# Experts' loop over single blocks, with the down product in three products of rounded parts

## The chip, the cores and the metric

One core of one Trainium2 chip. The metric is the device time of one execution in microseconds (us), lower is better. The kernel is launched once and computes the whole trunk.

## The reference

A trunk of two layers on 512 tokens of width 1024, all in float32. Layer 0 mixes by a Conformer convolution, layer 1 by dilated attention over a shared K/V. After each comes the part that this change touches, a mixture of 16 experts of hidden width 512, two of them for each token:

```python
a = jnp.einsum("td,edf->tef", t, w_gate)
u = jnp.einsum("td,edf->tef", t, w_up)
hid = jax.nn.silu(a) * u * gates[:, :, None].astype(t.dtype)
y = jnp.einsum("tef,efd->td", hid, w_down)
```

The kernel doesn't compute every expert for every token: it routes, gathers the rows of each expert, and adds the weighted results.

## The kernel before

**Blocks and pairs.** The tokens of each expert are cut into blocks of 128 slots. There are at least 16 blocks (one for each expert), and more where an expert has over 128 tokens. In this run layer 0 has 17 blocks and layer 1 has 16. `moe_sp`, `moe_pool`, `moe_act`, `moe_dve` and `moe_pe` hold what each engine does in order; the engines wait for each other by semaphores. The loop goes over pairs of blocks (block number 2i + b, with b = 0 or 1 also naming the buffer). The last pair stands behind the loop and is written apart; where `two` is 0 it holds one block. Layer 0 has 8 pairs in the loop, layer 1 has 7.

**One block.** Its rows (`xg[b]`, gathered by an indirect DMA of GpSimd) are transposed on TensorE. ScalarE rounds them to the type fp32r (`xgh`, "lead"), VectorE takes the remainder (`xgl`, "trail"). The same is done with the expert's gate and up weights: ScalarE copies `wg[b]` into `wgh` and `wu[b]` into `wuh` (one buffer each), in halves of 128x2048, and VectorE writes the remainder in place of the raw weight (`wgl[b]`, `wul[b]`). A product in rounded parts is then three matmuls of fp32r where there would be one of f32: high times high, high times low, low times high. `gate` and `up` are 24 such matmuls each, into banks 0 and 1. ScalarE takes the silu, VectorE multiplies (`hidden`), TensorE transposes the result into bank 2, and VectorE copies it to `hidT`. The **down product** is plain f32: 8 matmuls of 128x512, which the trace shows as 16 records:

```python
for ft in range(FT):
    ins = M.matmul(PS[3 + h][:, :], hidT[:, ft, :], wd[b][:, ft, h * 512:(h + 1) * 512],
                   start=ft == 0, stop=ft == FT - 1)
```

ScalarE copies banks 3 and 4 to `yst[b]` (`store_y`), and GpSimd scatters it to DRAM by an indirect DMA.

**Order on TensorE** in a pair (`pair` of `moe_pe`, L1878): gate 0, up 0, gate 1, transposed hidden 0, rows of the next block 0, up 1, down 0, transposed hidden 1, rows of the next block 1, down 1.

**Queues.** SP issues the weight loads of 2 MB each (`expert_loads`, L578) in the order gate, up, down of block 0, then of block 1, each behind a wait until the buffer's last product is done. GpSimd issues gather, scatter, gather, scatter, each behind its waits, and each after small operations of its own (L694, L699, L705, L708). Each engine, and each queue, takes its work in the order written.

**Before the loop**: routing writes the block lists; two gathers, the transposes of both blocks' rows, then gate 0. GpSimd clears the last pair's rows in DRAM from `zeros` (`clear`) behind the gathers of the second pair. **Behind the loop**: the last pair, whose result is spread by matmuls (`sum_rows`) and added to the residual.

Of the kernel before, what the change touches and what calls it, by code (L numbers as in the profile page):

```python
# [120 lines left out]
class Later:  # L121
# [6 lines left out]
    def at(self, n):  # L128
        return self.base + n


def build_program(nc, a):
# [7 lines left out]
    with ExitStack() as ctx:  # L140
# [131 lines left out]
        zeros = cut(SC, 2 * D, D)  # L272
        SUM_BANKS = (5, 7, 0, 1)
# [46 lines left out]
        col = rs(2 * NT)  # L320
        hr = rs(2 * NT, E)
        big = rs16(2 * NT * MAXC * E).rearrange("p (a b c) -> p a b c", a=2 * NT, b=MAXC)
        over = rs(MAXC - 1, E)
# [4 lines left out]
        match = rs(XB, MAXC - 1, E)  # L328
# [136 lines left out]
        spread_mm, spread_sb = Later(var_mm, KT), Later(sig_done, KT)  # L465
        y_added, y_cleared = Later(taps_done, len(BY_TAPS)), Later(sem("y_cleared"), 0)
# [14 lines left out]
        def _(sp):  # L481
# [66 lines left out]
            def moe_sp(l):  # L548
# [29 lines left out]
                def expert_loads(i, bs, uses):  # L578

                    for b in bs:  # L580
                        j = sp.value_load(blk_e[0:1, bass.ds(2 * i + b, 1)], min_val=0, max_val=E - 1) + l * E
                        for dst, name, s, used in ((wg, "w_gate", wg_in, gate_mm), (wu, "w_up", wu_in, up_mm), (wd, "w_down", wd_in, down_mm)):
                            sp.wait_ge(used[l], uses + b)
                            expert_load(l, j, b, dst, name, s)

                with sp.Fori(1, last) as i:
                    expert_loads(i, (0, 1), 2 * i - 1)
                expert_loads(last, (0,), 2 * before + 1)
                with sp.If(two > 0):
                    expert_loads(last, (1,), 2 * before + 1)  # L590
# [59 lines left out]
        def _(pool):  # L650
# [21 lines left out]
            def moe_pool(l):  # L672
# [56 lines left out]

# [4 lines left out]
                def pair(i, more):  # L734

                    if not isinstance(i, int):
                        stored(i)
# [49 lines left out]
        def _(act):  # L787
# [140 lines left out]
            def moe_act(l):  # L928
# [6 lines left out]
                def lead(src, dst, w_in, done, n):  # L935

                    act.wait_ge(w_in, n * 16)
                    for q in range(2):
# [3 lines left out]
                def gate_lead(b, n, used):  # L942
                    if used is not None:
                        act.wait_ge(gate_mm[l], used)
                    lead(wg[b], wgh, wg_in[l][b], gh_done[l], n)
# [6 lines left out]
                def rows_lead(b, n):  # L952

                    act.wait_ge(xgT_mm[l][b], n)
                    for q in range(2):
                        nc.scalar.activation(xgh[b][:, 4 * q:4 * q + 4, :], PS[ROW_BANKS[b][q]][:, :].rearrange("p (a b) -> p a b", a=4),
# [4 lines left out]
                for b in range(2):  # L961
                    rows_lead(b, 1)
# [4 lines left out]
                def pair(i, more):  # L967
                    def silu_gate(b):
                        act.wait_ge(gate_mm[l], 2 * i + (b + 1))
                        act.wait_ge(hid_done[l], 2 * i + (b + 1))  # L970
                        nc.scalar.activation(sil, PS[0][:, :], ACT.Silu).then_inc(sil_done[l], 1)

                    def store_y(b):
                        to = yst[b] if more else yst[0]
                        act.wait_ge(down_mm[l], 2 * i + (b + 1))
                        act.wait_ge(y_free[l], i + 1)
                        nc.scalar.activation(to[:, 0:512], PS[3][:, :], ACT.Copy)
                        nc.scalar.activation(to[:, 512:1024], PS[4][:, :], ACT.Copy).then_inc(y_done[l], 1)  # L978

                    silu_gate(0)  # L980
                    if more:
                        gate_lead(1, i + 1, 2 * i + 1)
                        up_lead(1, i + 1, 2 * i + 1)
                        silu_gate(1)
                        gate_lead(0, i + 2, 2 * i + 2)
                        rows_lead(0, i + 2)
                        up_lead(0, i + 2, 2 * i + 2)
                        store_y(0)
                        rows_lead(1, i + 2)
                        store_y(1)  # L990
                    else:
                        def copy_hidT(b):
                            act.wait_ge(hT_mm[l], 2 * i + (b + 1))
                            if b == 1:
                                act.wait_ge(down_mm[l], 2 * i + 1)
                            nc.scalar.activation(hidT.rearrange("p a b -> p (a b)"), PS[2][:, :], ACT.Copy).then_inc(hidT_done[l], 1)  # L996

                        with act.If(two > 0):
                            gate_lead(1, i + 1, 2 * i + 1)
                            up_lead(1, i + 1, 2 * i + 1)  # L1000
                            silu_gate(1)
                        copy_hidT(0)
                        act.wait_ge(spread_mm.sem, spread_mm.at(l + 1))
                        nc.scalar.activation(spread_w[0], PS[5][:, :], ACT.Copy).then_inc(spread_sb.sem, 1)
                        store_y(0)
                        with act.If(two > 0):
                            copy_hidT(1)
                            act.wait_ge(y_done[l], 2 * i + 2)
                            nc.scalar.activation(yst[1], yst[0], ACT.Copy)
                            nc.scalar.activation(spread_w[1], PS[5][:, :], ACT.Copy).then_inc(hidT_done[l], 1)  # L1010
                            act.wait_ge(hidT_done[l], 2 * i + 3)
                            nc.scalar.activation(spread_w[0], PS[6][:, :], ACT.Copy)
                            store_y(1)

                with act.Fori(0, last) as i:
                    pair(i, True)
                pair(last, False)
# [75 lines left out]
        def _(dve):  # L1093
# [369 lines left out]
            def moe_dve(l):  # L1463
# [12 lines left out]
                def up_trail(b, m):  # L1476
                    trail(wu[b], wuh, wul[b], uh_done[l], ul_done[l], m)

                def rows_trail(b, m):

                    for q in range(2):
                        dve.wait_ge(xh_done[l], 2 * m + (q + 1))
                        ins = V.tensor_tensor(xgl[b][:, 4 * q:4 * q + 4, :], PS[ROW_BANKS[b][q]][:, :].rearrange("p (a b) -> p a b", a=4),
# [3 lines left out]
                gate_trail(0, 0, [0])  # L1487
                mixing_weights(l)
                rows_trail(0, 0)
                two = dve.value_load(two_i[0:1, 0:1], min_val=0, max_val=1)  # L1490
                last = dve.value_load(last_i[0:1, 0:1], min_val=E // 2 - 1, max_val=(E + XB) // 2 - 1)
                gate_trail(0, 0, [1])
                rows_trail(1, 1)
# [16 lines left out]
                def pair(i, more):  # L1510
                    def hidden(b):
                        dve.wait_ge(sil_done[l], 2 * i + (b + 1))
                        dve.wait_ge(up_mm[l], 2 * i + (b + 1))
                        V.tensor_tensor(hid, PS[1][:, :], sil, ALU.mult).then_inc(hid_done[l], 1)

                    def copy_hidT(b):
                        dve.wait_ge(hT_mm[l], 2 * i + (b + 1))
                        if b == 1:
                            dve.wait_ge(down_mm[l], 2 * i + 1)
                        V.tensor_copy(hidT.rearrange("p a b -> p (a b)"), PS[2][:, :]).then_inc(hidT_done[l], 1)  # L1520

                    if more:
                        gate_trail(1, 2 * i + 1)
                        hidden(0)
                        up_trail(1, 2 * i + 1)
                        copy_hidT(0)
                        gate_trail(0, 2 * i + 2)
                        rows_trail(0, 2 * i + 2)
                        hidden(1)
                        copy_hidT(1)  # L1530
                        up_trail(0, 2 * i + 2)
                        rows_trail(1, 2 * i + 3)
                        dve.wait_ge(down_mm[l], 2 * i + 2)
                    else:
                        steps.wait()
                        for b in range(2):
                            place_last(b)
                        with dve.If(two > 0):
                            gate_trail(1, 2 * i + 1)
                        hidden(0)  # L1540
                        with dve.If(two > 0):
# [679 lines left out]
```

## Time and profile before

| | us |
|---|---|
| median of 3 runs (lowest, highest) | 1597.34 (1595.4, 1599.31) |
| the profiled execution, device time | 1596.6 |
| its span, first to last instruction | 1594.8 |
| TensorE busy in the span | 1530.2 (96%) |
| VectorE busy | 1077.8 (68%) |
| ScalarE busy | 677.4 (42%) |

The experts' loops take from 250 to 563 us (layer 0) and from 1257 to 1532 us (layer 1) of the span. Busy times overlap: an engine that is busy 96% of the span isn't idle for long anywhere, and a group's mean duration can be longer than the distance from one matmul to the next, since matmuls are pipelined.

### The profile page before, as it was taken

The page shows a single profiled execution, that of the slowest core. Times are in us where ns is not written, and L with a number is a line of the kernel's source. Part 1 is how long each engine was busy: PE and PEld are TensorE (multiplying, and loading weights), DVE is VectorE, ACT ScalarE, POOL GpSimd, SP SyncE. Part 2 cuts the span into 40 slices and gives each one's busy share as a digit, 9 for nine tenths or more (in the row PEclk, how much of TensorE's full clock was granted, in tenths as well). Part 3 has the DMA queues.
Part 4 walks back from the last instruction along what each step waited for, and adds up shares of the span by engine and source line. Part 5 has one row for each costly group of instructions (what it writes and reads, how often), then busy time and mean ns, then how long its engine had stood idle before and what let it go on. Part 6 is the DMA issues. An engine that isn't in the chain of part 4 may idle for free.

```text
span 1594.8 us, 19902 instructions
## 1 busy us (share of the span) xinstructions
PE 1530.2 (96%) x7320; PEld 1181.0 (74%) x7320; DVE 1077.8 (68%) x1327; ACT 677.4 (42%) x742; POOL 411.9 (26%) x351
## 2 busy tenths in 40 slices
PE   6989888999999989999999999999999799999997
PEld 5878676666666657888888888888888566666663
DVE  6997748555555579586767767586772955555566
ACT  4111636455555534423323241423333555555552
POOL 4000025222222217150513224150501522222220
PEclk9999989999999999999999999999999899999999
DMA  5233425888888863121212121221435578888873
GB/s 216 73 126 98 193 106 233 330 335 340 345 354 351 342 273 105 64 79 39 92 41 90 53 79 53 66 79 40 170 129 219 197 295 352 346 359 339 356 283 132
DMA packets 52535, 309.85 MB, mean 194 GB/s; under 512 B 10512, under 2 KB 16272, under 8 KB 38672
## 3 DMA queue, kind: packets, MB, share of 16 engines
q1 hardware_dynamic: 41840, 291.28, 46.6%
q0 software_dynamic: 9792, 16.80, 2.9%
q10 hardware_dynamic: 864, 1.26, 0.2%
q8 instruction: 24, 0.39, 0.1%
q14 instruction: 15, 0.12, 0.0%
HBM read 299.33 MB, written 28.84 MB: 206 GB/s over the span
## 4 chain that ended last, share of the span: by engine, by line
PE 78%; DVE 9%; DMA 8%; ACT 2%; issue 2%; SPq 0%; POOL 0%; DVEq 0%; ACTq 0%; POOLq 0%
PE PS L1913 12%; PE PS L2000 5%; PE PS L2002 5%; PE PS L2001 5%; PE PS L2085 3%; PE PS L1888 3%; DMA WR<-w_gate 3%; DMA WR<-w_up 3%; PE PS L2101 3%; PE PS L1892 3%; PE PS L1889 3%; PE PS L1875 3%; PE PS L1873 3%; PE PS L2016 3%; PE PS L2018 3%; PE PS L2017 3%
## 5 line engine op out<-in xcount | busy, mean ns | idle before, releaser
L1471 DVE TENSOR_TENSOR wgl<-WR,wgh 128x2048 fp32r<-128x2048 f32 x66 | 148.5, 2289 | 208.0 <-ACT wgh L940 206.9
L778 POOL TENSOR_TENSOR KQ<-rope_ab 64x512 f32<-64x512 f32 x96 | 173.6, 1809 | 364.8 <-DVE rope_ab L1583 361.2
L1913 PE MATMUL PS<-WR,SC 128*128 128x512 f32 x528 | 233.2, 594 | 2.6 <-ACT SC L996 1.3
L1025 ACT ACTIVATE wh<-wraw 128x1024 fp32r<-128x1024 f32 x76 | 80.3, 1058 | 249.5 <-PE PS L2002 248.7
L1913 PEld LDWEIGHTS PS<-WR,SC 128*128 128x128 f32 x528 | 98.8, 190 | 116.6 <-issue 114.5
L1471 DVE TENSOR_TENSOR wul<-WR,wuh 128x2048 fp32r<-128x2048 f32 x66 | 148.1, 2285 | 0.1
L940 ACT ACTIVATE wgh<-WR 128x2048 fp32r<-128x2048 f32 x66 | 122.4, 1904 | 60.4 <-DMA WR<-w_gate 60.4
L940 ACT ACTIVATE wuh<-WR 128x2048 fp32r<-128x2048 f32 x66 | 122.7, 1906 | 29.2 <-PE PS L1875 20.3
L1583 DVE TENSOR_TENSOR rope_ab<-PS,rope_sb 32x512 f32<-32x512 f32 x192 | 131.9, 687 | 2.6
L1888 PE MATMUL PS<-wgh,xgh 128*128 128x512 f32 x264 | 111.4, 422 | 1.0 <-DVE wgl L1471 1.0
L1565 DVE TENSOR_TENSOR wl<-wraw,wh 128x1024 fp32r<-128x1024 f32 x76 | 93.1, 1225 | 28.0 <-ACT wh L1025 26.3
L1873 PE MATMUL PS<-wuh,xgh 128*128 128x512 f32 x264 | 104.4, 395 | 0.0
L1889 PE MATMUL PS<-wgl,xgh 128*128 128x512 f32 x264 | 103.6, 392 | 0.0
L1875 PE MATMUL PS<-wuh,xgl 128*128 128x512 f32 x264 | 103.0, 390 | 0.0
L1874 PE MATMUL PS<-wul,xgh 128*128 128x512 f32 x264 | 102.7, 389 | 0.0
L1625 DVE RECIPROCAL rope_ab<-PS 64x512 f32<-64x512 f32 x16 | 53.7, 3359 | 61.8 <-PE PS L2101 61.6
L2000 PE MATMUL PS<-HQh,wh 128*128 128x512 f32 x192 | 76.3, 398 | 4.6 <-DVE HTl L1127 2.6
L708 POOL TENSOR_TENSOR idle<-ident_sb 128x1 f32<-128x1 f32 x30 | 34.2, 1140 | 165.4 <-ACT SC L978 165.4
L2016 PE MATMUL PS<-HTh,wh 128*128 128x512 f32 x192 | 76.2, 397 | 0.0
L2002 PE MATMUL PS<-HQh,wl 128*128 128x512 f32 x192 | 75.6, 394 | 0.0
L2001 PE MATMUL PS<-HQl,wh 128*128 128x512 f32 x192 | 75.4, 393 | 0.0
L2018 PE MATMUL PS<-HTh,wl 128*128 128x512 f32 x192 | 74.8, 390 | 0.0
(323 smaller groups left out, 3307.8 us busy)
## 6 DMA issues: line engine op xcount, KB each, us to landing
WR<-w_gate SPq DMA_DIRECT2D x33, 2048.0 KB, 12.1
WR<-w_up SPq DMA_DIRECT2D x33, 2048.0 KB, 16.7
WR<-w_down SPq DMA_DIRECT2D x33, 2048.0 KB, 8.3
wraw<-w_qkv SPq DMA_DIRECT2D x72, 512.0 KB, 3.3
WR<-w_in SPq DMA_DIRECT2D x8, 1024.0 KB, 4.9
xn_dram<-SC SPq DMA_DIRECT2D x8, 512.0 KB, 2.8
SC<-y_dram SPq DMA_DIRECT2D x8, 512.0 KB, 5.8
HT<-y_dram SPq DMA_DIRECT2D x8, 512.0 KB, 9.4
```

Source lines behind the costliest of these rows:

```text
L778: nc.gpsimd.tensor_tensor(to, cos, sin, ALU.add).then_inc(rope_done, 1)
L940: nc.scalar.activation(dst[:, kts, :], src[:, kts, :], ACT.Copy).then_inc(done, 1)
L1471: V.tensor_tensor(lo[:, kts, :], raw[:, kts, :], hi[:, kts, :].bitcast(F32), ALU.subtract).then_inc(done, 1)
L1583: ins = V.tensor_tensor(rope_ab[d:d + 32, 2 * (t % 2) + 1, :], src[s:s + 32, :], rope_t[s:s + 32, tab + 1, :], ALU.mult)
L1873: M.matmul(dst, xgh[b][:, kt, :], hi[:, kt, :], start=kt == 0, stop=False)
L1875: ins = M.matmul(dst, xgl[b][:, kt, :], hi[:, kt, :], start=False, stop=kt == KT - 1)
L1888: M.matmul(PS[0][:, :], xgh[b][:, kt, :], wgh[:, kt, :], start=kt == 0, stop=False)
L1889: M.matmul(PS[0][:, :], xgh[b][:, kt, :], wgl[b][:, kt, :], start=False, stop=False)
L1913: ins = M.matmul(PS[3 + h][:, :], hidT[:, ft, :], wd[b][:, ft, h * 512:(h + 1) * 512], start=ft == 0, stop=ft == FT - 1)
L2000: M.matmul(PS[t % 2][:, :], whk, hi[:, kt, :], start=kt == 0, stop=False)
L2001: M.matmul(PS[t % 2][:, :], whk, lo[:, kt, :], start=False, stop=False)
L2002: ins = M.matmul(PS[t % 2][:, :], wlk, hi[:, kt, :], start=False, stop=kt == KT - 1)
```

## The change

The loop's body becomes one block: number 2i + c, with c = 1 and 2 written out, so that each pass of the hardware loop still covers two blocks. In it, the down product of the block before is done in two halves of 512 columns, one ahead of this block's up product and one behind it. Each half is 12 matmuls of fp32r (high-high, low-high, high-low), in place of 4 of f32. The hidden rows are split (`hTh` by ScalarE, `hTl` by VectorE), and so is the down weight: its high half goes to `wdh`, one buffer for both halves of columns, and the remainder to `wdl[b]`, in place of `wd[b]`. With n blocks, blocks 0 to n-3 (17 blocks) or 0 to n-4 (16 blocks) get the split down product: 15 in layer 0 and 13 in layer 1. The last block of the loop and the last pair keep the f32 form.

Buffers, and one moved table (`match` made room for `hTl`); `wdh` lies over `zeros`, `hTh` over `hidT`:

```diff
+        wdh = at("wdh", 184, [P, FT, 512], F32R)
+        wdl = [at(f"wdl{b}", 112 + 16 * b, [P, FT, D], F32R) for b in range(2)]
+        hTh = at("hTh", 196, [P, FT, P], F32R)
...
+        hTl = at("hTl", 32 + o / 256, [P, FT, P], F32R)
```

SP: the down load of a block is issued one block later in the queue.

```diff
-                with sp.Fori(1, last) as i:
-                    expert_loads(i, (0, 1), 2 * i - 1)
-                expert_loads(last, (0,), 2 * before + 1)
...
+                gate_up_loads(1, 0, 1)
+                gate_up_loads(1, 1, 1)
+                down_load(1, 0, 1)
+                with sp.Fori(2, last) as i:
+                    gate_up_loads(i, 0, 2 * i - 1)
+                    down_load(i - 1, 1, 2 * i - 3)
+                    gate_up_loads(i, 1, 2 * i - 1)
+                    down_load(i, 0, 2 * i - 1)
```

GpSimd: the clears go ahead of the second pair's gathers; the wait for the stored rows stands in each scatter, and in ScalarE's copies, in place of `stored(i)` at the head of a pair.

```diff
                 def scatter(b, n):
+                    if not isinstance(n, int):
+                        pool.wait_ge(y_stored[l][b], n * 16)
...
                 for b in range(2):
+                    clear(b)
+                for b in range(2):
                     pool.wait_ge(gathered[l][b], 16)
                     gather(b, 1)
-                for b in range(2):
-                    clear(b)
```

ScalarE, one block:

```diff
+                def split_block(i, c):
+                    p, n = (c - 1) % 2, (c + 1) % 2
+                    act.wait_ge(hT_mm[l], 2 * i + c)
+                    nc.scalar.activation(hTh[:, :, :].rearrange("p a b -> p (a b)"), PS[2][:, :], ACT.Copy).then_inc(hTh_done[l].sem, 1)
+                    act.wait_ge(wd_in[l][p], (i + 1) * 16)
+                    if isinstance(i, int) and i == 0 and c == 1:
+                        act.wait_ge(y_cleared.sem, y_cleared.at(32 * (l + 1)))
+                    down_lead(0, i, p)
+                    silu_gate(i, c)
+                    gate_lead(n, i + 2, None, [0])
+                    act.wait_ge(down_half[l].sem, down_half[l].at(2 * i + c))
+                    down_lead(1, i, p)
+                    gate_lead(n, i + 2, None, [1])
+                    if not isinstance(i, int):
+                        act.wait_ge(y_stored[l][p], i * 16)
+                    nc.scalar.activation(yst[p][:, 0:512], PS[3][:, :], ACT.Copy)
+                    rows_lead(n, i + 2)
+                    up_lead(n, i + 2, 2 * i + (c + 1))
+                    act.wait_ge(down_mm[l], 2 * i + c)
+                    nc.scalar.activation(yst[p][:, 512:1024], PS[4][:, :], ACT.Copy).then_inc(y_done[l], 1)
```

VectorE, one block (ahead of the loop, `gate_trail(0, 0)` and `rows_trail(0, 0)` now stand in front of `mixing_weights`):

```diff
+                def split_block(i, c, between=None):
+                    n, m = (c + 1) % 2, 2 * i + (c + 1)
+                    dve.wait_ge(hTh_done[l].sem, hTh_done[l].at(2 * i + c))
+                    V.tensor_tensor(hTl[:, :, :].rearrange("p a b -> p (a b)"), PS[2][:, :],
+                                    hTh[:, :, :].rearrange("p a b -> p (a b)").bitcast(F32), ALU.subtract).then_inc(hidT_done[l], 1)
+                    down_trail(0, i, c)
+                    gate_trail(n, m, [0])
+                    down_trail(1, i, c)
+                    gate_trail(n, m, [1])
+                    hidden(i, c)
+                    rows_trail(n, m)
+                    up_trail(n, m, [0])
+                    if between is not None:
+                        between()
+                    up_trail(n, m, [1])
```

TensorE: half a down product, one block, and the order around the loop (`transpose_rows(1, 1)` was ahead of gate 0).

```diff
+                def split_down(h, i, c):
+                    b, to = (c - 1) % 2, PS[3 + h][:, :]
+                    pe.wait_ge(dh_done[l].sem, dh_done[l].at(4 * i + (2 * c - 1 + h)))
+                    if h == 0:
+                        pe.wait_ge(hidT_done[l], 2 * i + c)
+                        pe.wait_ge(y_done[l], 2 * i + c)
+                    for ft in range(FT):
+                        M.matmul(to, hTh[:, ft, :], wdh[:, ft, :], start=ft == 0, stop=False)
+                        M.matmul(to, hTl[:, ft, :], wdh[:, ft, :], start=False, stop=False)
+                    pe.wait_ge(dl_done[l].sem, dl_done[l].at(4 * i + (2 * c - 1 + h)))
+                    for ft in range(FT):
+                        ins = M.matmul(to, hTh[:, ft, :], wdl[b][:, ft, h * 512:(h + 1) * 512], start=False, stop=ft == FT - 1)
...
+                def split_block(i, c):
+                    gate(i, c)
+                    transpose_rows((c + 1) % 2, i + 2)
+                    split_down(0, i, c)
+                    up(i, c)
+                    split_down(1, i, c)
+                    transpose_hidden(i, c)
+
+                gate(0, 0)
+                transpose_rows(1, 1)
+                up(0, 0)
+                transpose_hidden(0, 0)
+                with pe.Fori(0, before) as i:
+                    for c in (1, 2):
+                        split_block(i, c)
+                split_block(before, 1)
+                transpose_rows(1, before + 2, 1)
+                down(before, 1)
```

The rows of all blocks in the loop now go through the same two banks (`banks=0`); the last pair's block 1 keeps its own.

## Rows read from the trace of the kernel before

**Rows 1.** The page: busy times of the engines, and DMA share and rate by slice.
```profile
PE 1530.2 (96%) x7320; PEld 1181.0 (74%) x7320; DVE 1077.8 (68%) x1327; ACT 677.4 (42%) x742; POOL 411.9 (26%) x351
DMA  5233425888888863121212121221435578888873
GB/s 216 73 126 98 193 106 233 330 335 340 345 354 351 342 273 105 64 79 39 92 41 90 53 79 53 66 79 40 170 129 219 197 295 352 346 359 339 356 283 132
```

**Rows 2.** Windows, one for each pair: width, busy us by engine, clock, DMA share, GB/s.
```profile
399.80:438.60 38.80, 38.69 (x152) 26.78 (x153) 22.66 (x17) 21.34 (x20) 9.48 (x13) 1.00 0.84 348
438.60:478.00 39.40, 38.99 (x152) 26.75 (x152) 22.65 (x17) 21.32 (x20) 9.50 (x13) 1.00 0.87 356
1407.90:1446.60 38.70, 38.70 (x153) 26.91 (x154) 22.55 (x17) 21.34 (x19) 9.59 (x14) 1.00 0.82 343
```

**Rows 3.** The chain of waits in a pair: start us, us, what.
```profile
421.58 1.83 PE PS L1892 x8
...
430.26 6.87 PE PS L1913 x16
437.13 0.47 PE PS L1904 x4
437.60 0.90 PE PS L1862 x8
...
451.36 16.59 DMA WR<-w_gate
```

**Rows 4.** Timeline, TensorE, last down product of each loop: start us, us, operation.
```profile
555.53 7.11 PE L1913 MATMUL PS<-WR,SC 128*128 128x512 f32 x16
1524.96 7.10 PE L1913 MATMUL PS<-WR,SC 128*128 128x512 f32 x16
```

**Rows 5.** Timeline, ScalarE, in one pair.
```profile
438.53 1.08 ACT L956 ACTIVATE xgh<-PS 128x512 fp32r<-128x512 f32 x2
446.24 0.59 ACT L978 ACTIVATE SC<-PS 128x512 f32<-128x512 f32 x1
446.85 1.28 ACT L971 ACT_TABLE_LOAD   x1
451.73 3.71 ACT L940 ACTIVATE wgh<-WR 128x2048 fp32r<-128x2048 f32 x2
```

**Rows 6.** Timeline, VectorE, in one pair.
```profile
453.67 4.49 DVE L1471 TENSOR_TENSOR wgl<-WR,wgh 128x2048 fp32r<-128x2048 f32 x2 [9.74 <-ACT wgh L940]
458.08 0.68 DVE L1514 TENSOR_TENSOR SC<-PS,SC 128x512 f32<-128x512 f32 x1
474.34 1.28 DVE L1483 TENSOR_TENSOR xgl<-PS,xgh 128x512 fp32r<-128x512 f32 x2
```

**Rows 7.** Windows of 2 us inside a pair (columns as in group 2).
```profile
401.75:403.70 1.95, 1.95 (x6) 0.80 (x5) 1.95 (x1) 0.00 (x0) 1.80 (x2) 1.00 1.06 454
...
427.10:429.05 1.95, 1.95 (x10) 1.60 (x10) 0.00 (x0) 0.50 (x1) 1.34 (x3) 1.00 0.98 420
...
434.90:436.85 1.95, 1.95 (x6) 0.69 (x5) 1.89 (x4) 1.95 (x2) 0.00 (x0) 1.00 0.00 0
```

**Rows 8.** Weight loads between 321 and 560 us, issue to landing.
```profile
DMA to landing us min/median/max: 7.5/15.9/17.7
```

**Rows 9.** Timeline, GpSimd: small operations and issues, beside and without VectorE's work.
```profile
253.72 2.19 POOL L721 COPY HTQ<-HTQ 128x1 uint32 x1
...
401.91 2.89 POOL L709 DMA_INDIRECT y_dram<-SC,HTQ  x1 [0.15 <-issue]
404.81 0.19 POOL L694 COPY HTQ<-HTQ 128x1 uint32 x1
...
408.82 1.01 POOL L709 DMA_INDIRECT y_dram<-SC,HTQ  x1 [0.51 <-issue]
```

**Rows 10.** Timeline at both loops' starts: TensorE, then GpSimd.
```profile
248.57 1.97 PE L1862 MATMUL PS<-ident_sb,SC 128*128 128x128 f32 x8 [1.17 <-DMA SC<-xn_dram,HTQ]
250.20 0.78 PE L1888 MATMUL PS<-wgh,xgh 128*128 128x512 f32 x1
1256.74 0.48 PE L1888 MATMUL PS<-wgh,xgh 128*128 128x512 f32 x1
243.65 1.04 POOL L700 DMA_INDIRECT SC<-xn_dram,HTQ  x1 [0.17 <-issue]
```

**Rows 11.** DMA issues between 252.6 and 252.8 us: the gather of a second-pair block.
```profile
SC<-xn_dram,HTQ POOLq DMA_INDIRECT x1, 12.9
```

More of the change, by code:

```diff
@@ L960, in moe_act @@
                 up_lead(0, 1, None)
-                for b in range(2):
-                    rows_lead(b, 1)
+                rows_lead(0, 1)
                 act.wait_ge(routed.sem, routed.at(l, 1))
@@ L965, in moe_act @@
                 last = act.value_load(last_i[0:1, 0:1], min_val=E // 2 - 1, max_val=(E + XB) // 2 - 1)
[L967 to L971, printed above, removed]
+                before = act.value_load(last_i[0:1, 1:2], min_val=E // 2 - 2, max_val=(E + XB) // 2 - 2)
@@ new lines, in moe_act @@
+                silu_gate(0, 0)
+                gate_lead(1, 1, 1)
+                rows_lead(1, 1)
+                up_lead(1, 1, 1)
+                for c in (1, 2):
+                    split_block(0, c)
+                with act.Fori(1, before) as i:
+                    for c in (1, 2):
+                        split_block(i, c)
+                split_block(before, 1)
+                rows_lead(1, before + 2, 1)
+                act.wait_ge(down_mm[l], 2 * before + 2)
+                act.wait_ge(y_stored[l][1], before * 16)
@@ L982, in pair @@
+                    with act.If(two > 0):
                         gate_lead(1, i + 1, 2 * i + 1)
                         up_lead(1, i + 1, 2 * i + 1)
[L984 to L989, printed above, removed]
-                        store_y(1)
[L991 to L1013, printed above, removed]
@@ L1019, in _ @@
+                last_pair(last)
             moe_act(0)
@@ L1508, in place_last, with hidden @@
                         V.tensor_tensor(to, to, part, ALU.add).then_inc(spread_set.sem, 1)
[L1510 to L1522, printed above, removed]
+                def hidden(i, c):
+                    dve.wait_ge(sil_done[l], 2 * i + (c + 1))
+                    dve.wait_ge(up_mm[l], 2 * i + (c + 1))
+                    V.tensor_tensor(hid, PS[1][:, :], sil, ALU.mult).then_inc(hid_done[l], 1)
@@ new lines, in copy_hidT @@
+                def copy_hidT():
+                    dve.wait_ge(hT_mm[l], 2 * before + 2)
+                    V.tensor_copy(hidT.rearrange("p a b -> p (a b)"), PS[2][:, :]).then_inc(hidT_done[l], 1)
+                gate_trail(1, 1)
+                hidden(0, 0)
+                rows_trail(1, 1)
+                up_trail(1, 1)
+                with dve.Fori(0, before) as i:
+                    for c in (1, 2):
+                        split_block(i, c)
+                split_block(before, 1, copy_hidT)
@@ L1523, in pair, with last_pair @@
+                rows_trail(1, 2 * before + 3, 1)
+                def last_pair(i):
+                    steps.wait()
+                    for b in range(2):
+                        place_last(b)
+                    with dve.If(two > 0):
                         gate_trail(1, 2 * i + 1)
-                        hidden(0)
+                    hidden(i, 0)
+                    with dve.If(two > 0):
                         up_trail(1, 2 * i + 1)
-                        copy_hidT(0)
-                        gate_trail(0, 2 * i + 2)
@@ L1528, in pair @@
[L1528 to L1541, printed above, removed]
-                            up_trail(1, 2 * i + 1)
-                            hidden(1)
-                        for n in range(NT):
-                            add_stored(n, l)
-                        dve.wait_ge(y_added.sem, y_added.at((l + 1) * NT))
-                        with dve.If(two > 0):
-                            for n in range(NT):
-                                for h in range(2):
-                                    dve.wait_ge(sum_mm[l].sem, sum_mm[l].at(2 * n + h + 1))
-                                    add_sum(n, h).then_inc(sum_add[l].sem, 1)
@@ L1553, in moe_dve @@
-                with dve.Fori(0, last) as i:
-                    pair(i, True)
-                pair(last, False)
+                        hidden(i, 1)
+                    for n in range(NT):
+                        add_stored(n, l)
+                    dve.wait_ge(y_added.sem, y_added.at((l + 1) * NT))
+                    with dve.If(two > 0):
+                        for n in range(NT):
+                            for h in range(2):
+                                dve.wait_ge(sum_mm[l].sem, sum_mm[l].at(2 * n + h + 1))
+                                add_sum(n, h).then_inc(sum_add[l].sem, 1)
@@ L1556, in moe_dve @@
+                last_pair(last)
                 return two
@@ L1963, in moe_pe, with gate @@
-                with pe.Fori(0, last) as i:
-                    pair(i, True)
-                pair(last, False)
+                def gate(i, c):
+                    b = c % 2
+                    if c > 0:
+                        pe.wait_ge(sil_done[l], 2 * i + c)
+                    for kt in range(KT):
+                        if kt % half == 0:
+                            pe.wait_ge(xh_done[l], 4 * i + (2 * c + kt // half + 1))
+                            pe.wait_ge(gl_done[l], 4 * i + (2 * c + kt // half + 1))
+                        M.matmul(PS[0][:, :], xgh[b][:, kt, :], wgh[:, kt, :], start=kt == 0, stop=False)
+                        M.matmul(PS[0][:, :], xgh[b][:, kt, :], wgl[b][:, kt, :], start=False, stop=False)
+                    pe.wait_ge(xl_done[l], 2 * i + (c + 1))
+                    for kt in range(KT):
+                        ins = M.matmul(PS[0][:, :], xgl[b][:, kt, :], wgh[:, kt, :], start=False, stop=kt == KT - 1)
+                    ins.then_inc(gate_mm[l], 1)
@@ new lines, in down @@
+                def down(i, b):
+                    pe.wait_ge(wd_in[l][b], (i + 1) * 16)
+                    pe.wait_ge(hidT_done[l], 2 * i + (b + 1))
+                    pe.wait_ge(y_done[l], 2 * i + (b + 1))
+                    for h in range(2):
+                        for ft in range(FT):
+                            ins = M.matmul(PS[3 + h][:, :], hidT[:, ft, :], wd[b][:, ft, h * 512:(h + 1) * 512],
+                                           start=ft == 0, stop=ft == FT - 1)
+                    ins.then_inc(down_mm[l], 1)
@@ L1967, in _ @@
+                last_pair(last)
             moe_pe(0)
```

235 lines of the change are left out of this document (124 added, 111 removed).

## The prediction

> **What bounds the kernel now.** I read the page first: TensorE is busy 96% of the span, and in the experts' slices the DMA engines stand at eight tenths with 330 to 359 GB/s [rows 1]. Then windows, one for each pair of blocks: TensorE is busy for 38.7 to 39.0 us of 38.7 to 39.4, at a granted clock of 1.00; VectorE for 22.7, ScalarE for 21.3 [rows 2]. The chain of waits says what a pair is made of: 8 matmuls of fp32r in 1.83 us (0.228 us each), the transposed hidden rows 0.47, the next rows 0.90, and the f32 down product 6.87, or 7.1 where it stands behind a wait [rows 3, 4]. A DMA appears in it only now and then: a gate weight, 16.59 us from issue to landing, holds ScalarE's rounding [rows 3], and with it some pairs last 39.4 instead of 38.7. So the loop is bound by TensorE, and a block costs 2 x 5.48 (gate, up) + 6.98 (down) + 0.47 + 0.90 = 19.3 us. I also looked at what must grow: ScalarE's and VectorE's operations [rows 5, 6], the DMA rate inside a pair [rows 7, 8], and GpSimd's small operations [rows 9].
>
> **The down product.** Removed: 6.98 us. Added: 24 matmuls x 0.228 = 5.46, same shape as gate's. The trace has no fp32r product with `wdh`, so bounds: if each half pays the start behind a wait, some 0.1 each, 5.7; if an fp32r matmul here went no faster than half an f32 one (6.87 / 16 = 0.43), 10.3; below, 24 x 0.22 = 5.3, since no row has it faster. I take 5.46 and put the waits in a term of their own. The gain is 1.52 a block, on the path, for 15 + 13 = 28 blocks: **42.6 us**.
>
> **TensorE's waits.** A block will have 16 waits instead of 13, and the down product in two pieces. Old pairs lose 38.7 - 38.6 = 0.1 to this. I take 0.15 a block (bounds 0 and 0.5), so a block lasts 5.48 + 0.90 + 2.73 + 5.48 + 2.73 + 0.47 + 0.15 = **17.95 us**, against 19.35 to 19.7 now.
>
> **Does the rest fit into 17.95?** Walk one block, with 0 at the end of the transposed hidden rows of the block before. TensorE: gate to 5.5, rows to 6.4, first half of down to 9.2, up to 14.7, second half to 17.4, hidden transposed to 17.95.
> ScalarE: leads are 3.71 for two halves, a PSUM copy 0.59 (pitch 0.5), rows 1.08 [rows 5]. The up weight's lead and the last copy of the block before run to about 1.2; `hTh` to 1.7; down lead to 3.6; silu at 5.5 to 6.1; gate lead, first half, to 7.9; behind the wait for the first half of down (9.2), down lead to 11.0; gate lead to 12.9; copy, rows to 14.5; behind up (14.7), the up lead to 18.4; last copy to 18.9, which is 0.95 of the next block: it closes. Sum 14.6, and one table load of 1.28 [rows 5] a pass, hidden in the gap between 3.6 and 5.5. Were it two, silu ends at 6.7, still harmless.
> VectorE: trails are 4.49 for two halves, 0.68 for an operation on PSUM, rows 1.28 [rows 6]. The up trails end at 4.0; `hTl` 4.6; down trail 6.9; gate trail (lead at 7.9) 10.2; down trail (11.0) 13.3; gate trail 15.6; hidden 16.2; rows 17.5; up trails (leads at 16.6, 18.4) to 21.9, which is 4.0 again. Sum 3 x 4.49 + 1.28 + 2 x 0.68 = 16.1 of 17.95. TensorE needs the down trail at 8.2 (spare 1.3), the up trails at 9.2 (5), hidden at 17.4 (1.2), the gate trail at 17.95 (2.3). The thinnest cover is 1.2 us; each us beyond it costs 28 us in all. The old table copy to `hidT` is gone, `hTl` takes its place.
> So ScalarE's added 3.7 + 0.5 and VectorE's added 4.5 lie beside TensorE's work, and I cost them at nothing.
>
> **Loads.** All three of a block's weights still move; SP's queue is past nothing that has to come earlier: gate at 5.5, up at 14.7, down at 17.4, in order of time. A pair moves 348 GB/s x 38.8 us = 13.5 MB [rows 2]. In the 14 windows of 2 us from 401.8 to 429.0 the engines stand at a share of 1 and move 405 to 460 GB/s, mean about 428; near 435 they are empty [rows 7], because four of a pair's six loads wait for the second half of it. At 428 a pair needs 31.5 us, a block 15.8; with what lies between landings I reckon 17.0, under 17.95. Each load may take about 18 us from its issue until ScalarE wants it (gate: 5.5 to 6.1 of the next block, 18.5; up 17.9; down 20). The longest now is 17.7 [rows 8], behind a backlog of three loads that the new order, spread over the block, doesn't build. So the wait for the gate weight goes too: old pairs of layer 0 last 312.4 / 8 = 39.05 on average [rows 4, 10], 0.35 over 38.7; this is in the end points below.
>
> The Trainium skill, "SBUF — State Buffer", summary of rules for kernel authors, says to reckon with about 358 GB/s between HBM and SBUF. By it a pair would need 37.7 us and a block 18.9, and DMA would take TensorE's place; the trace's 428 over 27 us disagrees, though no slice of 40 us has more than the rule gives, hence rival 1.
>
> **Ends of the loops.** Layer 0 now: gate 0 starts at 250.2 behind the second block's rows [rows 10], the last pair at 555.53 + 7.0 = 562.5 [rows 4]. New: gate 0 needn't wait for the second rows, 248.7; rows, up 0, then one idle us for `hidden`; first block of the loop at 262.2; 15 x 17.95 = 269.3; then rows 0.9, a wait of 0.9 for `hidT` (VectorE's first up trail is ahead of it) and 7.0 of f32. That gives 540.3, plus the start's gather. The second pair's gather is issued behind two clears: from 243.65 + 1.04 [rows 10] six small steps of 2.2 and issues of 1.0 to 2.9 [rows 9] bring it to about 261.5, where it was at 252.7. Its landing took 12.9 then behind the down loads [rows 11], it may take 5 to 13 now; TensorE wants the rows at 268.6. Stall 0 to 6, I take 2.5: 542.8, so **19.7** saved. Layer 1: 1256.74 to 1532.0 now [rows 4, 10]; new first block at 1269.5, 13 x 17.95 = 233.4, stall 1, 8.8: 1512.7, **19.3** saved. What follows the loops is as before: the last loads are issued at the same distance from the last pair.
>
> **Sum.** 1596.6 - 39 = 1557.6, in the profiled execution's own time; it lies 0.7 under the median of the runs, so **1558**. With waits at 0 and no stalls it would be 1549; with waits at 0.5 a block and stalls of 6, 1573.
>
> **Rivals.**
> 1. DMA paces the block. For: the share is already 0.84 to 0.87 [rows 2], and no slice has over 359 GB/s [rows 1]. Against: the windows at 428 [rows 7]. If 359 were the limit, 13.5 MB take 37.6 us, 18.8 a block: 28 x 0.85 = 24 over the forecast, 1582.
> 2. GpSimd starves, the slower side. Its small operations take 0.19 us alone and 2.2 under a trail, an issue 1.0 and 2.9 [rows 9]. VectorE's trails grow from 9 to 13.5 us a block, so each step may meet one: four steps and two issues, 4 x 2.2 + 5.8 + gaps = 16, just inside a block. If each step waited for two trails (4.5), 4 x 4.5 + 5.8 = 23.8 a block: the rows and `yst` come late, and 28 x (23.8 - 19.4) = 123 are lost: 1720. It decides from 19.4 us a block on, 3.4 a step. Against: at 253.72 VectorE was busy all the while and the step took 2.19.
> 3. The products don't pay: 24 fp32r matmuls take what 16 f32 records take (0.29 each). Then only the stalls go, about 5 us: 1592. Against: gate's 0.228, with operands laid out the same way.
>
> The Trainium skill, "SBUF — State Buffer", section "Who interferes with whom", has it that a VectorE instruction with two SBUF inputs and a GpSimd instruction that reads SBUF exclude each other for the whole instruction. The trace agrees as to one trail (2.19 against 0.19); it speaks against this change as far as rival 2 goes, whose two trails in a row no row shows.
>
> **How the numbers follow.** Forecast 0.72, rival 1 (or another 0.3 to 1 us a block) 0.16, rival 2 0.05, rival 3 0.04, and 0.03 for a failed cover that costs more than all gains. The forecast's own range is 1549 to 1570; with part of rival 1 it is 1549 to 1577. A difference under 0.2% (3 us) can't be told from none. Faster 0.90, same 0.03, slower 0.07.
>
> **What would show it.** Pairs of 35.9 us in windows from the third block on, TensorE idle in them for under 0.3; down's fp32r matmuls at 0.228 pitch; DMA share about 0.92 at 375 GB/s; VectorE at 32 us a pair. A stall of TensorE at the transposed hidden rows says that VectorE has no cover; ScalarE waiting for weights says rival 1; TensorE waiting for gathered rows in mid-loop, or ScalarE for stored rows, says rival 2. I am wrong if a pair takes over 37.

## The result, and the profile after

The changed kernel takes **1560.3 us** (median of 4 runs, 1559.8 to 1560.7), against 1597.6 for the kernel before: a ratio of 0.976, 95% interval 0.975 to 0.9775. The forecast was 1558, with a range of 1549 to 1577. The profiled execution's span is 1558.6 us, 36.2 less than before.

The page of the changed kernel, the lines that answer to [rows 1]:

```profile
PE 1489.0 (96%) x7544; PEld 1223.9 (79%) x7544; DVE 1200.9 (77%) x1383; ACT 773.2 (50%) x813; POOL 488.3 (31%) x338
...
DMA  5242517899999663121212121212256389999973
GB/s 194 95 134 83 213 52 287 347 373 370 377 393 391 253 262 95 55 81 40 94 40 81 54 81 54 81 54 67 72 199 246 115 335 367 387 380 383 365 279 124
```

TensorE is still busy 96% of a shorter span; VectorE and ScalarE have taken up the roundings, and the DMA digits in the experts' slices went from 8 to 9. Windows, one for each two blocks, answer to [rows 2]:

```profile
391.94:427.59 35.65, 35.65 (x170) 29.77 (x169) 31.58 (x21) 28.13 (x25) 16.80 (x12) 1.00 0.95 380
427.59:463.25 35.66, 35.66 (x170) 29.77 (x169) 31.59 (x21) 28.16 (x25) 16.80 (x12) 1.00 0.97 393
...
1379.42:1415.07 35.65, 35.65 (x170) 29.77 (x169) 31.59 (x21) 28.14 (x25) 16.80 (x12) 1.00 0.95 377
```

Two blocks take 35.65 us, 17.83 a block, and TensorE isn't idle in them at all. Every split block but the first of each loop lasts 17.82 or 17.83. The long pairs that waited for a gate weight are gone. The chain of waits in one block holds TensorE alone (start us, us, what; the answer to [rows 3]):

```profile
395.61 1.82 PE PS L1954 x8
397.43 0.88 PE PS L1927 x8
...
400.17 0.91 PE PS L1990 x4
408.39 0.91 PE PS L1990 x4
409.30 0.47 PE PS L1966 x4
```

VectorE's timeline in the same block shows how it fits between: the hidden product (L1561) ends at 408.17, and TensorE begins the transposes at 409.30 in the chain. VectorE's only gaps are those in brackets, 1.17 and 0.88 us:

```profile
395.85 0.68 DVE L1572 TENSOR_TENSOR hTl<-PS,hTh 128x512 fp32r<-128x512 f32 x1
396.45 2.28 DVE L1567 TENSOR_TENSOR wdl<-WR,wdh 128x2048 fp32r<-128x2048 f32 x1
399.90 2.29 DVE L1520 TENSOR_TENSOR wgl<-WR,wgh 128x2048 fp32r<-128x2048 f32 x1 [1.17 <-ACT wgh L963]
403.07 2.29 DVE L1567 TENSOR_TENSOR wdl<-WR,wdh 128x2048 fp32r<-128x2048 f32 x1 [0.88 <-ACT wdh L996]
405.28 2.28 DVE L1520 TENSOR_TENSOR wgl<-WR,wgh 128x2048 fp32r<-128x2048 f32 x1
407.48 0.69 DVE L1561 TENSOR_TENSOR SC<-PS,SC 128x512 f32<-128x512 f32 x1
```

Weight loads between 391 and 500 us, from issue to landing. Where it was 15.9 and at most 17.7 [rows 8], it is 11.0 and 12.1, with the issues spread over the block:

```profile
DMA to landing us min/median/max: 8.0/11.0/12.1
```

And the ends of the loops, TensorE's timeline: the first gate product of layer 0, the first transposed hidden rows, and the f32 product behind the split blocks (it answers to [rows 4] and [rows 10]):

```profile
251.20 0.79 PE L1950 MATMUL PS<-wgh,xgh 128*128 128x512 f32 x1 [0.69 <-ACT xgh L979]
...
266.42 0.75 PE L1966 MATMUL PS<-ident_sb,SC 128*128 128x128 f32 x4 [1.27 <-DVE SC L1561]
...
537.04 7.11 PE L1975 MATMUL PS<-WR,SC 128*128 128x512 f32 x16 [1.59 <-DVE SC L1587]
```

### The profile page after: what moved, and what is told of

Same layout as the page of the kernel before. It is cut to its first block, busy times and chain, and to the rows that moved or that the text cites. A ratio compares the mean times of both kernels' runs of the same rounds, so it can differ in the third digit from the quotient of the medians.

```text
span 1558.6 us, 20726 instructions
## 1 busy us (share of the span) xinstructions
PE 1489.0 (96%) x7544; PEld 1223.9 (79%) x7544; DVE 1200.9 (77%) x1383; ACT 773.2 (50%) x813; POOL 488.3 (31%) x338
## 4 chain that ended last, share of the span: by engine, by line
PE 85%; DVE 10%; issue 1%; DMA 1%; ACT 1%; DVEq 0%; SPq 0%; ACTq 0%; POOLq 0%
PE PS L2087 5%; PE PS L2089 5%; PE PS L2088 5%; PE PS L1950 4%; PE PS L1951 4%; PE PS L1954 4%; PE PS L2172 4%; PE PS L1939 3%; PE PS L1937 3%; PE PS L1938 3%; PE PS L1986 3%; PE PS L1987 3%; PE PS L2188 3%; PE PS L1990 3%; PE PS L2103 3%; PE PS L2105 3%
## 5 line engine op out<-in xcount | busy, mean ns | idle before, releaser
L1567 DVE TENSOR_TENSOR wdl<-WR,wdh 128x2048 fp32r<-128x2048 f32 x56 | 128.0, 2286 | 24.3 <-ACT wdh L996 24.3
L996 ACT ACTIVATE wdh<-WR 128x2048 fp32r<-128x2048 f32 x56 | 107.4, 1919 | 35.0 <-PE PS L1990 35.0
L1950 PE MATMUL PS<-wgh,xgh 128*128 128x512 f32 x264 | 107.8, 408 | 1.4 <-ACT xgh L979 1.4
L734 POOL TENSOR_TENSOR idle<-ident_sb 128x1 f32<-128x1 f32 x30 | 20.8, 694 | 260.9 <-ACT SC L1017 248.7
L1986 PE MATMUL PS<-wdh,hTh 128*128 128x512 f32 x224 | 91.1, 407 | 0.0
L1987 PE MATMUL PS<-wdh,hTl 128*128 128x512 f32 x224 | 88.2, 394 | 0.0
L735 POOL DMA_INDIRECT y_dram<-SC,HTQ x30 | 79.4, 2647 | 5.3 <-issue 5.3
```

The costliest lines, as they stand in the source:

```text
L1950: M.matmul(PS[0][:, :], xgh[b][:, kt, :], wgh[:, kt, :], start=kt == 0, stop=False)
L1986: M.matmul(to, hTh[:, ft, :], wdh[:, ft, :], start=ft == 0, stop=False)
L1987: M.matmul(to, hTl[:, ft, :], wdh[:, ft, :], start=False, stop=False)
```

## The experiments

Each was timed beside the kernel before on one chip. The changed kernel was run again beside the later ones (e5 to e10), since they differ from it by a few us; for e1 to e4 it stands at 1560.3 from the first chip.

**e1, the order alone.** The down product goes back to f32, in the new place:

```diff
-                        M.matmul(to, hTh[:, ft, :], wdh[:, ft, :], start=ft == 0, stop=False)
-                        M.matmul(to, hTl[:, ft, :], wdh[:, ft, :], start=False, stop=False)
...
+                        ins = M.matmul(to, hidT[:, ft, :], wd[b][:, ft, h * 512:(h + 1) * 512], start=ft == 0, stop=ft == FT - 1)
```

> The new order and the new queues, but the down product in f32 as before (two halves of 4 f32 matmuls, no hTh, hTl, wdh, wdl). Theory (the gain is the cheaper product, the order only hides its roundings): a block goes from 17.83 to 17.83 + 6.92 - 5.46 = 19.3 us, 28 blocks give back 41 us: about 1601, a little over the kernel before, whose pairs average 19.5 a block but whose loops start 2 to 3 us faster. Rival (the order itself saves, by ending the waits for weights and for the copy of the hidden rows): 1585 or less.

1592.7 us, ratio to before 0.9973 (0.9963 to 0.9982). The chain of e1 in one block:

```profile
400.27 0.47 PE PS L1956 x4
...
407.09 3.44 PE PS L1976 x8
...
416.00 3.43 PE PS L1976 x8
419.43 0.47 PE PS L1956 x4
```

From 400.27 to 419.43, from one set of transposed hidden rows to the next, a block lasts 19.16. So the cheaper product is worth 19.16 - 17.83 = 1.33 us a block (6.87 of f32 against 5.54), 37 us in 28 blocks, and the order, which ends the waits for weights and lets the f32 product run without a start behind a wait, 19.52 - 19.16 = 0.36, 10 us. In layer 0 e1 also lost 4.6 us once, in its first block: it came to the third block's rows at about 267.6 and they weren't there.

```profile
270.12 1.69 PE L1917 MATMUL PS<-ident_sb,SC 128*128 128x128 f32 x8 [2.51 <-DMA SC<-xn_dram,HTQ]
```

Most of the gain is the product's, as the theory had it. By the medians e1 is 4.1 us under the kernel before and the changed kernel is 37.3 under it, so the product brings some 33 and the order alone 4, where the theory had e1 at 4 over. The blocks' 10 us of the order don't all arrive: 4.6 of them go in that first block. The split product in the old order of pairs was not tried.

**e2, two of the three products.** It leaves out the low-high product of the split blocks:

```diff
-                        M.matmul(to, hTl[:, ft, :], wdh[:, ft, :], start=False, stop=False)
```

> Leaves out the low-high product of the down projection (8 of its 24 matmuls a block), all else as in the changed kernel, hTl included: shows what bounds a block next. TensorE then needs 17.83 - 1.82 = 16.0 us. Theory A (VectorE, 15.8 busy, with its order comes next): 16.1 to 16.5 a block, 28 x 1.3 to 1.7 less, 1513 to 1524. Theory B (DMA paces from the 17.0 that I reckoned from landings): 17.0 a block, 1537. Theory C (DMA can do no more than the 380 to 393 GB/s of now): 17.5 to 17.8 a block, 1551 to 1560.

1531.5 us, 16.73 a block, where TensorE's own work is 16.0. A window of two blocks, and the landing of weight loads issued between 280 and 310 us, and between 430 and 460:

```profile
382.50:416.00 33.50, 33.03 (x154) 26.53 (x152) 31.60 (x21) 28.17 (x25) 20.91 (x12) 1.00 0.99 403
```
```profile
DMA to landing us min/median/max: 7.8/10.8/11.5
...
DMA to landing us min/median/max: 13.1/17.0/17.9
```

The chain in it runs through VectorE and ScalarE (start us, us, what):

```profile
421.61 0.68 DVE hTl L1572
422.29 2.21 DVE wdl L1567
...
424.55 1.21 PE PS L1989 x4
425.76 0.02 issue
425.79 1.93 ACT wdh L996
```

The number lies between A (16.1 to 16.5) and B (17.0), and in neither; by the total B is even a little nearer. It is the chain that speaks for A's mechanism: no DMA is in it, and VectorE, busy 15.8 of 16.73, sets the pace together with the order in which it and ScalarE take the halves. What A had too small is the waiting between the two. C fell: the DMA engines moved 403 GB/s. B is half right. DMA doesn't end the chain, but its share is 0.99, and the median landing grew from 10.8 us to 17.0 in some 9 blocks, 0.7 a block; after that it stayed at 17.0 (460 to 490 us). By this growth DMA's own pace is some 17.4 us a block (an estimate from these two medians), and a longer loop would have used up the 18 us that a load may take. So behind TensorE's 17.83 stand DMA at about 17.4, which this loop is too short to feel, and VectorE at about 16.7. In the changed kernel the same medians stay between 9.2 and 12.0 over the whole loop.

**e3 and e5, VectorE's cover.** One more VectorE instruction ahead of the hidden product, over 280 columns (1.90 us) or 110 (0.84 us):

```diff
+                    V.reciprocal(PS[7][:, 0:280], hTh[:, :, :].rearrange("p a b -> p (a b)")[:, 0:280].bitcast(F32))
                     hidden(i, c)
```

> Adds one VectorE instruction (a reciprocal over 128x280, about 1.9 us by the 3.36 us of 64x512) ahead of the hidden product in each of the 28 split blocks. Theory (VectorE's cover ahead of the transposed hidden rows is 1.1 us, nothing else): each block grows by 1.9 - 1.1 = 0.8, 22 us in all: 1582. Rival (the walk's spare isn't the real one; since VectorE is then busy 17.7 of 17.83, queued waits add up): 1.9 a block or more, 1613. Rival (VectorE runs ahead and absorbs it): 1561.

> As e3, but a reciprocal over 128x110, about 0.75 to 0.8 us (from e3's 1.90 us for 280 columns). From e3 the cover is 1.83 - 1.09 = 0.75, where the walk had 1.1: theory (the cover is 0.75 to 0.85): blocks of 17.83 to 17.9, total 1560 to 1562. Rival (no cover: VectorE's time counts in full once it is near its limit): 0.75 a block, 1581.

e3: 1592.95 us, blocks of 18.82 and 19.0, 18.92 on average (the first of layer 0 20.78, with a wait of 1.67 for gathered rows in it). e5: 1563.1 us beside 1558.4 for the changed kernel on that chip, blocks of 17.82 to 17.99. TensorE waits at the transposed hidden rows (e3; waits in us, times, longest):

```profile
PE PS L1967 <- DVE SC L1561: 8.0, 11, 0.7
```

An instruction in a row takes some 0.08 less than its own time, so e3 added 1.82 and the block grew by 1.09; e5 added 0.76 and it grew by 0.06. Both give a cover of **0.7 us**, where the walk had 1.2 and TensorE's first transpose comes 1.1 behind VectorE's end. The weight loads (PEld) show why: the hidden rows are what the transposes load as weights, and in the changed kernel this load begins at 408.91, 0.74 behind VectorE's 408.17. In e3 it waits for VectorE (start us, us, and the idle time before it; first the changed kernel, then e3):

```profile
408.91 0.67 PEld L1966 LDWEIGHTS PS<-ident_sb,SC 128*128 128x128 f32 x4
...
396.83 0.56 PEld L1967 LDWEIGHTS PS<-ident_sb,SC 128*128 128x128 f32 x4 [1.15 <-DVE SC L1561]
```

Beyond the cover VectorE's time is paid in every block. The first theory of each run has the mechanism, with the cover too large: for e3 it said 0.8 a block and 1582, and 1.09 and 1593 came. In e5 the blocks make 1.6 of the 4.7 us over the changed kernel. In the profiled execution most of the rest is at the end of layer 0's loop: the copy for the f32 product came 0.7 later, and the product took 8.80 us instead of 7.11, at a granted clock of 0.50 from 537.5 to 540.5. In layer 1 it took 7.10.

**e4, the loads in the old order.** SP's queue again takes gate, up, down of a pair's block 0, then of block 1:

```diff
...
+                with sp.Fori(1, last) as i:
+                    for b in range(2):
+                        gate_up_loads(i, b, 2 * i - 1)
+                        down_load(i, b, 2 * i - 1)
...
```

> The changed kernel with SP's queue in the old order: gate, up, down of block 2i, then of block 2i+1. The down load of block 2i can only be issued at the end of block 2i+1's pass, and the gate load of block 2i+3's buffer stands behind it: 12 us later than now. Theory (the queue order is what keeps the loads off the path): gate weight lands 7 us too late once in a pair, half of it made good: 3.5 to 7 us a pair, 14 pairs: 50 to 95 us, 1610 to 1655. Rival (18 us of slack for a load that lands in 11 is enough): 1560 to 1565.

1646.3 us, ratio to before 1.031 (1.028 to 1.033): slower than before the change, with every other part of it in. Two of the waits between 300 and 500 us:

```profile
DVE wgl L1515 <- ACT wgh L958: 57.4, 10, 9.2
ACT wgh L958 <- DMA WR<-w_gate: 38.6, 9, 5.8
```

ScalarE waits for the gate weight, VectorE for ScalarE, and the blocks last about 21 us. The theory's 50 to 95 us came as 86 over the changed kernel. The split alone isn't the change; the queue that issues the down load a block later belongs to it.

**e7 and e8, the ends of the loops.** e7 moves VectorE's copy ahead of the up trails, its three register loads (2.3 us) behind the first up trail, and the first hidden product between the halves of a gate trail. e8 adds filler matmuls at the start. The last of e7's three edits, and e8's:

```diff
...
-                gate_trail(1, 1)
+                gate_trail(1, 1, [0])
                 hidden(0, 0)
+                gate_trail(1, 1, [1])
...
+                fill(8)
                 transpose_rows(0, 1)
+                fill(4)
```

> The changed kernel, with VectorE's copy of the hidden rows for the loop's last f32 down product ahead of both halves of the up trail, VectorE's three register loads behind the first up trail, and the first hidden product between the halves of the second block's gate trail. Theory (the ends of the loops are a chain through VectorE): the wait of 1.59 us ahead of the f32 product goes in both layers (3.2), the loops start 0.7 and 1.7 us earlier, unless the gathered rows of the third block are late then: 1554 to 1557. Rival (other waits end at the same time): within 1 us of the changed kernel.

> e7, and 8 matmuls of bf16 into a free bank ahead of the first rows' transposes and 4 behind them. In the changed kernel TensorE's granted clock was 0.50 from 251.2 to 255.2 us, behind an idle stretch, and 9 matmuls took 0.43 instead of 0.23 us there. Theory (with no idle stretch the clock stays up): 1.8 us less than e7 in layer 0, 1552 to 1555. Rival (the fillers themselves are on the path, or the first gather and not TensorE sets the start): same as e7 or 1 us more.

> The changed kernel once more beside these three, to compare on one chip: 1560 to 1561.

e7 took 1559.1 us, e8 1559.5, the changed kernel beside them 1558.4: nothing gained. TensorE's timeline of e7 shows why. It came to the transposes earlier and then waited at the down product of the first block, which lasted 19.92 instead of 17.93:

```profile
265.49 0.75 PE L1967 MATMUL PS<-ident_sb,SC 128*128 128x128 f32 x4 [0.85 <-DVE SC L1561]
...
273.93 0.47 PE L1987 MATMUL PS<-wdh,hTh 128*128 128x512 f32 x1 [1.31 <-issue]
```

At the start VectorE is the bound, and what I took from one place I put ahead of another (`hTl` at 273.15 in e7, 271.88 in the changed kernel). e8's filler made no difference to the time that can be measured, and its trace shows what it did:

```profile
246.14 2.74 PE L1933 MATMUL PS<-c_sb 128*128 128x384 bf16 x8 [2.03 <-issue]
248.67 1.30 PE L1928 MATMUL PS<-ident_sb,SC 128*128 128x128 f32 x8
...
250.65 0.50 PE L1957 MATMUL PS<-wgh,xgh 128*128 128x512 f32 x1
```

The gate product then ran at a granted clock of 1.00, where e7's first ones ran at 0.50. But the filler came behind TensorE's idle 2.03 us and not in it, ran at 0.50 itself, and stood ahead of the transposes for 2.5 us. From the start of a routing product that both have (`HTQ,c_sb`) to the first transposed hidden rows it is 30.8 us in e8 (232.84 to 263.60) and 31.0 in e7 (234.47 to 265.49). So it is the rival's first half: the filler is on the path, and costs what it gives back. The moved copy was still to be seen by itself, which led to e6.

**e6, the copy alone.**

```diff
+                    if between is not None:
+                        between()
                     up_trail(n, m, [0])
-                    if between is not None:
-                        between()
                     up_trail(n, m, [1])
```

> The changed kernel, with nothing moved but VectorE's copy of the hidden rows for the loop's last f32 down product, now ahead of both halves of the up trail. In e7 that wait went from 1.59 to 0.23 us, but the first block of each loop became 2.1 us longer. Theory (e7's start ate the gain of its end): 2 x 1.36 = 2.7 us less than the changed kernel, 1555.5 to 1556. Rival (the gain is given back behind the loop, where the last pair waits for the later up trail or the stored rows): within 1 us of it.

1555.3 us (1554.4 to 1556.5), beside 1559.3 (1557.4 to 1560.3) for the changed kernel: the fastest version here that has all three products. The f32 product behind the split blocks now waits 0.23 us instead of 1.59:

```profile
532.77 7.11 PE L1975 MATMUL PS<-WR,SC 128*128 128x512 f32 x16 [0.23 <-ACT SC L1017]
```

That accounts for 2.7 of the 4.0 us; the rest is no more than the difference between runs of one kernel: in the profiled executions e6's loop also starts 2.0 us earlier (248.53 against 250.50). The ratios to before (0.9741, 0.9727 to 0.9754, and 0.9761, 0.9748 to 0.9775) only just overlap.

**e10, GpSimd's cover.** Three small operations instead of one ahead of each gather and scatter:

```diff
-                        nc.gpsimd.tensor_tensor(idle[:, :], ident[:, 0:1], ident[:, 0:1], ALU.mult)
+                        for k in range(3):
+                            nc.gpsimd.tensor_tensor((idle, spare[:, 6:7], spare[:, 5:6])[k][:, :], ident[:, 0:1], ident[:, 0:1], ALU.mult)
```

> The changed kernel with three small GpSimd operations instead of one ahead of every gather and scatter of a block: 4 more a block, 0.2 to 2.2 us each. GpSimd waits 8.6 of 17.83 us a block for the stored rows, a gather lands some 12 and a scatter some 7 us ahead of need. Theory (it has that much cover): no change, 1558 to 1561. Rival 2 of the prediction (its steps each meet a trail, and the rows come late): over 5 us slower.

> The changed kernel beside these two, on the same chip: 1558 to 1561.

1557.9 us beside 1559.3: no change. GpSimd's timeline, one issue in the changed kernel, then e10:

```profile
393.94 2.90 POOL L735 DMA_INDIRECT y_dram<-SC,HTQ  x1 [0.16 <-issue]
...
392.78 0.69 POOL L736 TENSOR_TENSOR idle<-ident_sb 128x1 f32<-128x1 f32 x1 [8.65 <-ACT SC L1019]
393.43 2.39 POOL L736 TENSOR_TENSOR spare<-ident_sb 128x1 f32<-128x1 f32 x2
395.97 1.02 POOL L737 DMA_INDIRECT y_dram<-SC,HTQ  x1 [0.15 <-issue]
```

Its two extra steps took 2.39 us together, and the issue behind them 1.02 instead of the 2.90 it takes in the changed kernel. Both wait out the same trail of VectorE: it ends at 395.6 in e10, the steps at 395.8; it ends at 395.9 in the changed kernel, the issue at 396.8. So more steps don't mean more waiting. It still idles for 8.65 us a block.

## Why the prediction was right, point by point

**What bounds the kernel**: right. TensorE, before and after; the experts' loops gave 18.5 + 18.1 us of the span's 36.2, the stages between them took 0.5 more and those behind them 0.1 less.

**The down product**: 1.52 a block was forecast, e1 has 1.33. I took the mean of 6.87 and 7.1; the 7.1 holds a start behind a wait, which belongs to the order. The rest is on the new side, where I had 5.46 and 5.54 came. The term is 37 us and not 42.6.

**TensorE's waits and the old pairs' stalls**: 17.95 a block was forecast, 17.83 measured. The parts of the chain, 5.49 + 0.88 + 2.77 + 5.44 + 2.78 + 0.47, add up to all of it, so the 0.15 for waits was nothing. The gain against the old average of 19.52 is 1.69 a block and 47 us in all, 10 of them from the order. That is 3.4 over the forecast's 44, and the ends of the loops kept 6 more than forecast (below). That the total came within 2.3 us of 1558 is in part luck: two errors of opposite sign.

**The rest fits into a block**: right; the walk's times hold to a few tenths. I had the gate trail's first half end at 10.2, `hidden` at 16.2 and the up trails at 4.0; in the block from 391.94 they end at 10.2, 16.2 and 4.0 (409.28 + 4.48 - 391.94 - 17.83). Only the thinnest cover was too large: 0.7 and not 1.2 (e3, e5), because the walk set VectorE's end against the first transpose and not against its weight load.

**Loads**: right that TensorE keeps the lead, and that 18 us of slack would do. The share is 0.95 to 0.97 for the 0.92 I named. My 17.0 a block for DMA was low: e2's growing landings put it at about 17.4. The Trainium skill's 358 GB/s ("SBUF — State Buffer", summary of rules for kernel authors) is not this kernel's limit: 377 to 393 GB/s go through in the loop, and 403 in e2. (The prediction says that no slice of the kernel before had more than the rule gives; one had 359.) Rival 1 didn't come about.

**Ends of the loops**: the direction was right, the parts weren't. 28 blocks x 1.69 would be 47 us, 36 arrived: 11 us stay at the starts and ends. By the forecast's own numbers it was 28 x (19.52 - 17.95) = 44, of which 39 were to arrive, so 5. This term was sized at half of what it was. (The sum's upper bound of 1573 doesn't come out of its terms either: 0.35 more a block and stalls of 6 in both layers give 1576.) In layer 0 the gate product began at 251.2 and not at 248.7. The stage ahead ran 1.5 us later in this execution (it is as early as before in others), and behind an idle stretch of 2.03 us the granted clock was 0.50 from 248.5 to 255 us. The first 9 matmuls of the gate product took 0.43 instead of 0.23 us there, 1.8 in all:

```profile
251.20:253.00 1.80, 1.80 (x4) 1.49 (x5) 1.73 (x6) 1.00 (x2) 1.29 (x3) 0.50 0.54 182
...
257.00:259.00 2.00, 2.00 (x12) 1.69 (x12) 2.00 (x2) 0.17 (x1) 0.98 (x1) 1.00 1.07 451
```

The first transposed hidden rows ended at 267.2, for 262.2 forecast. In layer 1, where the clock stayed at 1.00, a wait that no term had shows instead, for VectorE's trail of the up weight:

```profile
1246.69 0.50 PE L1937 MATMUL PS<-wuh,xgh 128*128 128x512 f32 x1 [1.29 <-DVE wul L1520]
```

The stall for gathered rows (2.5 and 1 us) didn't come. The gather was issued at 255.2 and not at 261.5, since most of GpSimd's small steps there took 0.2 us and not 2.2, and the landing of the pair's two gathers took 13.7 us (median), so the first rows were there at about 270 (an estimate). TensorE, late itself, wanted them at 272.5. e1, whose TensorE was there at 267.6, has the stall. The wait for `hidT` was 1.59 for 0.9, because a half of the up trail was ahead of the copy, as the prediction said, and also the rows' trail ahead of that. The sum was 542.8 for the end of layer 0's loop, 544.0 measured.

**Rival 2** (GpSimd starves): its steps did take up to 1.9 us in the loop, but it waits 8.6 us a block, and e10 shows that steps in a row share one trail. This agrees with the Trainium skill ("SBUF — State Buffer", section "Who interferes with whom"), and bounds what the rule costs here: one trail for a run of steps, not one for each. **Rival 3**: didn't come about, the split product runs at 5.54 / 24 = 0.23 us a matmul.

## What to carry to other kernels

When a loop is bound by one engine, write down one turn as a walk, every engine with its ends in the frame of the turn: it gave the period within 1% and named the instruction with the least cover. Read a cover up to the first use of the data on the waiting engine, which for TensorE can be a weight load: here 1.1 us to the first transpose were 0.74 to its weight load, and added instructions gave 0.7. Measure it so before you fill it. A cheaper product in a software pipeline may pay only with the queue order that belongs to it: without that, this change loses 3% (e4). Sum the starts and the ends of a pipelined loop on their own; here they kept a quarter of what the blocks gained.

## What the runs showed of the hardware

Small GpSimd operations beside VectorE's trails don't add up: two took 2.39 us together, and an indirect DMA's issue fell from 2.90 to 1.02 us when it came behind them. The DMA engines held 403 GB/s over 33 us (e2) with a share of 0.99. TensorE's granted clock stood at 0.50 from 248.5 to 255 us at the start of layer 0's loop, behind 2.03 us in which it was idle. Filler behind that stretch ran at 0.50 itself, and the products after it at 1.00 (e8): the slow time moved and didn't shrink. At the end of layer 0's loop, behind waits of 2.3 to 2.4 us, the f32 product took 8.80 us in e2 and e5, partly at 0.50, and 7.10 in e3 at 1.00; why is open.
